# A hybrid decoder step on one core: order of loads, state products and sample work around the SSD chunks, and where the gathered rows lie

## The reference

```python
xn = _rmsnorm(x, norm_mix)
z, xbc, dt_raw, u = split(xn @ w_in)                    # 1024, 1536, 16, 1024 columns
xbc, new_conv = _causal_conv(xbc, conv_prefix, conv_w, conv_b)
y, new_ssm = _ssd_chunked(xs, dt, -exp(a_log), bm, cm, d_ssd, ssm_h0, chunk)   # 16 heads x 64, state 128
y_ssd = _rmsnorm(y * silu(z), ssd_norm)
y_s5, new_re, new_im = _s5_group(u, ...)                # recurrence, gelu, then y * sigmoid(y @ w_glu + b_glu), norm
x = x + concatenate([y_ssd, y_s5]) @ w_out
x = x + _hier_moe(_rmsnorm(x, norm_ffn), ...)           # 4 groups x 8 experts, 2 experts for each token
# inside a chunk c of the SSD part:
y_diag = einsum(cb * Lmat * dt, x)                      # products within the chunk
y_off  = einsum(C, h_prev, exp(cs))                     # from the state before the chunk
h      = decay * h + states                             # the state handed on
# inside the expert part:
h = silu(t @ w_gate[e]) * (t @ w_up[e]);  out += gates[:, e] * (h @ w_down[e])
```

## Time and profile before

| | us |
|---|---|
| median of 3 runs | 1091.96 (1091.92 to 1096.05) |
| the profiled execution, its own time | 1091.92 |
| its span in the trace | 1090.1 |
| PE busy | 982.3 (90%) |
| DVE busy | 451.7 (41%) |
| POOL busy | 332.9 (31%) |
| ACT busy | 308.8 (28%) |

### The profile page before, as it was taken

How to read it: one execution, slowest core, us unless ns; L and a number is a source line. 1 busy time by engine, 2 the same in 40 slices (tenths; PEclk the granted TensorE clock), 3 DMA queues, 4 the chain that set the end, 5 groups by cost and what they waited for, 6 DMA issues and landing times.

```text
span 1090.1 us, 17000 instructions
## 1 busy us (share of the span) xinstructions
PE 982.3 (90%) x6438; PEld 695.0 (64%) x6439; DVE 451.7 (41%) x674; ACT 308.8 (28%) x597; POOL 332.9 (31%) x534
## 2 busy tenths in 40 slices
PE   6999999999999997999999999999878778987881
PEld 5889789786776786998865555555444444544440
DVE  6999875533456998862341111111101001111103
ACT  3026223632324352231232223222211121222123
POOL 1000888888204993000012222222221111221110
PEclk9999999999999898999899999999999999999996
DMA  6674271120198534356399999999999999999954
GB/s 263 126 146 74 42 144 40 43 74 4 33 289 203 191 95 154 127 199 264 131 332 394 394 389 398 382 402 399 390 393 398 391 412 408 412 409 411 424 241 163
DMA packets 73564, 277.54 MB, mean 255 GB/s; under 512 B 36952, under 2 KB 38872, under 8 KB 56496
## 3 DMA queue, kind: packets, MB, share of 16 engines
q1 hardware_dynamic: 63020, 252.67, 63.1%
q0 software_dynamic: 8720, 19.86, 6.8%
q10 hardware_dynamic: 1780, 4.41, 1.1%
HBM read 260.17 MB, written 25.61 MB: 262 GB/s over the span
## 4 chain that ended last, share of the span: by engine, by line
PE 67%; DMA 21%; DVE 8%; issue 1%; ACT 1%; SPq 1%; ACTq 0%; POOLq 0%; POOL 0%; DVEq 0%
PE ps L658 20%; DMA sb_arena<-w_up 20%; PE ps L1026 8%; PE ps L1040 7%; PE ps L923 7%; PE ps L1019 7%; PE ps L993 2%; PE ps L777 2%; PE ps L690 1%; PE ps L803 1%; PE ps L828 1%; PE ps L746 1%; DVE sb_y_lo L1730 1%; PE ps L824 1%; DVE sb_arena L1749 1%
## 5 line engine op out<-in xcount | busy, mean ns | idle before, releaser
L658 PE MATMUL ps<-sb_arena 128*128 128x264 f32 (+1 forms) x1152 | 269.1, 395 | 9.6 <-DMA sb_arena<-wi 8.8
L658 PEld LDWEIGHTS ps<-sb_arena 128*128 128x128 f32 x1152 | 220.2, 193 | 58.6 <-DMA sb_arena<-wi 8.5
L1917 DVE TENSOR_TENSOR sb_s5b<-sb_s5b,ps 128x256 f32<-128x256 f32 x36 | 22.3, 620 | 416.2 <-PE ps L1026 416.2
L1026 PE MATMUL ps<-sb_arena 128*64 128x256 f32 x1152 | 134.6, 387 | 23.7 <-DMA sb_arena<-w_up 23.7
L1019 PE MATMUL ps<-sb_arena 128*64 128x256 f32 x1152 | 132.7, 383 | 19.6 <-DMA sb_arena<-w_gate 15.4
L1040 PE MATMUL ps<-sb_arena 128*64 128x512 f32 x576 | 131.5, 598 | 20.5 <-DVE sb_arena L1921 20.5
L1019 PEld LDWEIGHTS ps<-sb_arena 128*64 128x64 f32 x1152 | 84.0, 138 | 79.2 <-DMA sb_arena<-w_gate 25.5
L1026 PEld LDWEIGHTS ps<-sb_arena 128*64 128x64 f32 x1152 | 84.0, 139 | 70.6 <-DMA sb_arena<-w_up 30.4
L1370 ACT ACTIVATE sb_kxf<-ps,sb_gate_of 64x512 f32<-64x512 f32 x36 | 24.5, 682 | 309.9 <-PE ps L1040 309.9
L1040 PEld LDWEIGHTS ps<-sb_arena 128*64 128x64 f32 x576 | 39.2, 136 | 89.7 <-issue 60.8
L614 POOL COPY sb_idc<-sb_tok_of 64x1 int32 x36 | 6.4, 179 | 291.1 <-DMA sum_scr<-sb_kxf,sb_rwc 273.5
(11 more groups left out here) (308 smaller groups left out, 1275.9 us busy)
## 6 DMA issues: line engine op xcount, KB each, us to landing
sb_arena<-w_gate SPq DMA_DIRECT2D x32, 2048.0 KB, 33.0
sb_arena<-w_up SPq DMA_DIRECT2D x32, 2048.0 KB
sb_arena<-w_down SPq DMA_DIRECT2D x32, 2048.0 KB
sb_arena<-wi SPq DMA_DIRECT2D x28, 512.0 KB, 4.0
sb_arena<-w_out SPq DMA_DIRECT2D x4, 2048.0 KB, 7.8
sb_arena<-ssm_in POOLq DMA_DIRECT2D x8, 512.0 KB, 9.2
sb_arena<-wglu SPq DMA_DIRECT2D x8, 512.0 KB, 5.8
o_ssm_s<-sb_arena POOLq DMA_DIRECT2D x8, 512.0 KB, 3.9
```

The source lines that it names most:

```text
L658: last = mm(ps[:, b0 + h, 0:t1 - t0], ring[w % 3][:, k, :], src[:, k, t0:t1], start=k == 0, stop=k == KD - 1)
L1026: last = mm(ps[64 * r:64 * r + 64, 1, 0:256], xt[:, k, :], Wu[s][:, k, 256 * r:256 * r + 256], start=k == 0, stop=k == KD - 1)
L1917: V.tensor_tensor(hh.rearrange("p (j c) -> p c j", j=2), sg.rearrange("p (c j) -> p c j", j=2), ps[:, 1, 0:256].rearrange("p (c j) -> p c ...
```

## The change

It has seven parts, which the prediction calls by these letters.

- A. The gather targets `xg[i]` lie in partitions 0 to 63 for every i (before, odd i had partitions 64 to 127), and so do the rows of `yo`.
- B. On SP, `toeplitz(1)` stands before ring 14, and `toeplitz(2)` and `toeplitz(3)` before ring 15.
- C. On SP, `y_store(1)` stands before the wait for the first store and `y_load(0)`.
- D. On POOL, all eight sample loads stand behind the load of `bc_scr` (before, four of them stood ahead of it and two behind the second store of y). DVE waits for four loads at once.
- E. On PE, `state_outputs(0, 8)` stands after wide(24) instead of after wide(25); wide tile 27 uses bank 0; wide(29) stands behind `ssd_c(4)`; some waits go or move with that.
- F. On ACT, the gelu reads with a stride and writes in a row (before, the other way round), and four squares stand one tile later.
- G. On DVE, the scaling of `Hs` stands directly ahead of the addition to the state; the additions of rounds 0 to 7 stand in chunk 1 and those of 8 to 15 in chunk 2; two of the four sample steps that stood ahead of the wait for `y_mm` in chunk 4 stand behind it; in the tail, `root_inverse(1)` and both `scale_s5` stand before `project_out(3)`.

```diff
-        xg = [part(4288 + 1024 * i, D, p=(T * (i % 2), T * (i % 2) + T)) for i in range(RING)]
+        xg = [part(4288 + 1024 * i, D, p=(0, T)) for i in range(RING)]
@@
-        yo = [kxf[T * u:T * u + T, D + 1024 * u:D + 1024 * u + 1024] for u in range(2)]
+        yo = [kxf[0:T, D + 1024 * u:D + 1024 * u + 1024] for u in range(2)]
@@ SP
             toeplitz(0)
+            toeplitz(1)
             ring_load(14)
-            toeplitz(1)
-            ring_load(15)
             toeplitz(2)
             toeplitz(3)
-            for w in range(16, 22):
+            for w in range(15, 22):
...
+            y_store(1)
             sp.wait_ge(y5_st[0], 16 * 9)
             y_load(0)
-            y_store(1)
@@ POOL
+            pl.wait_ge(ea_out, 1)
+            pl.wait_ge(y5_mm, 16)
-            pl.wait_ge(y5_mm, 8)
-            for b in range(4, NS):
-                pl.dma_start(h0b[b], hin[b]).then_inc(h0s_ld[1], 16)
-            pl.wait_ge(ea_out, 1)
-            pl.wait_ge(y5_mm, 16)
...
-            for b in range(2):
-                pl.dma_start(h0b[b], hin[b]).then_inc(h0s_ld[0], 16)
+            for b in range(NS):
+                pl.dma_start(h0b[b], hin[b]).then_inc(h0s_ld[b // 4], 16)
             pl.wait_ge(bc_ld, 16)
-            pl.wait_ge(h0s_ld[0], 32)
-            pl.wait_ge(y5_st[1], 16 * 9)
-            for b in range(2, 4):
-                pl.dma_start(h0b[b], hin[b]).then_inc(h0s_ld[0], 16)
@@ PE
             wide(24)
+            state_outputs(0, 8)
             ssd_a(2)
+            pe.wait_ge(y5_ev, 8)
             ssd_b(2)
             ssd_y_off(2)
             wide(25)
-            pe.wait_ge(yo_ev, 4)
-            state_outputs(0, 8)
             ssd_c(2)
             state_outputs(8, 8)
...
             wide(28)
-            pe.wait_ge(yo_ev, 8)
-            wide(29)
             ssd_c(4)
-            for w in range(30, 36):
+            for w in range(29, 36):
@@ ACT
-                act_(yg[:, i, 0:NP_].rearrange("p (m j) -> p j m", j=J),
-                     yraw[:, i, 0:NP_].rearrange("p (j m) -> p j m", j=J), ACT.Gelu_apprx_tanh)
+                act_(yg[:, i, 0:NP_].rearrange("p (m j) -> p m j", j=J),
+                     yraw[:, i, 0:NP_].rearrange("p (j m) -> p m j", j=J), ACT.Gelu_apprx_tanh)
...
@@ DVE (the loop over chunks, written out)
                     else:
+                        tt(hs, hs, bc(dE[:, c, 1, 8 * g:8 * g + 8], 2, HD), ALU.mult)
                         last = V.tensor_tensor(hs, hs, pg, ALU.add)
                 last.then_inc(st_ev, 1)
-                if c == 2:
-                    s5_add(8)
+                for rd in range(8 * c - 8, 8 * c) if c in (1, 2) else ():
+                    dv.wait_ge(y5_mm, rd + 1)
...
@@ DVE, tail
             root_square(1)
-            project_out(3)
             root_inverse(1)
             scale_s5(0)
+            scale_s5(1)
+            project_out(3)
             project_out(4)
-            scale_s5(1)
```

More of the change, by code:

```diff
@@ L869, in _ @@
             ssd_a(4)
-            pe.wait_ge(wide_free[1], 14)
             ssd_b(4)
@@ L1217, in _ @@
             z_evac(20)
-            for c in range(4):
+            for c in range(5):
                 b_tokens(c)
@@ L1276, in _ @@
                         high_part(0, ySSD, PF_GSSD, k)
+                if w == 33:
                     for k in range(4, KD):
@@ L1634, in _ @@
             Ug = U[:, 0:G5 * UC].rearrange("p (g c) -> p g c", g=G5)
-            def s5_add(first):
-                for rd in range(first, first + 8):
-                    dv.wait_ge(y5_mm, rd + 1)
-                    o = Ug[:, 4 * rd:4 * rd + 4, 0:YC]
-                    V.tensor_tensor(o, o, ps[:, 2 + rd % 2, 0:4 * WIN].rearrange("p (q c) -> p q c", q=4)[:, :, 0:YC],
-                                    ALU.add).then_inc(y5_ev, 1)
-            def off_diagonal(c, n):
-                for g in range(2):
+            for c in range(5):
+                t0, n = CH[c]
+                dv.wait_ge(sa_mm, c + 1)
+                tt(cbm[0:n, :, 0:n], ps[0:n, 7, 0:256].rearrange("p (g l) -> p g l", g=2)[:, :, 0:n],
+                   bc(tri[0:n, 0:n], 1, 2), ALU.mult)
+                for q in range(2):
+                    tt(xdt[0:n, 8 * q:8 * q + 8, :], ps[0:n, 4 + q, :].rearrange("p (h d) -> p h d", d=HD),
+                       bc(dtv[0:n, c, 8 * q:8 * q + 8], 2, HD), ALU.mult)
+                dv.wait_ge(de_out, 1)
+                V.tensor_tensor(xde[0:n], xdt[0:n], bc(dE[0:n, c, 2, :], 2, HD), ALU.mult).then_inc(sa_evd, 1)
+                for g in range(2) if c else ():
                     dv.wait_ge(yo_mm, 2 * c - 1 + g)
@@ L1687, in _ @@
                     else:
+                        tt(hs, hs, bc(dE[:, c, 1, 8 * g:8 * g + 8], 2, HD), ALU.mult)
                         last = V.tensor_tensor(hs, hs, pg, ALU.add)
                 last.then_inc(st_ev, 1)
-                if c == 2:
-                    s5_add(8)
-                if c == 3:
-                    for b in range(2):
-                        sample_c(b)
-                if c == 4:
-                    for b in range(6, NS):
-                        sample_c(b)
+                for rd in range(8 * c - 8, 8 * c) if c in (1, 2) else ():
+                    dv.wait_ge(y5_mm, rd + 1)
+                    o = Ug[:, 4 * rd:4 * rd + 4, 0:YC]
+                    V.tensor_tensor(o, o, ps[:, 2 + rd % 2, 0:4 * WIN].rearrange("p (q c) -> p q c", q=4)[:, :, 0:YC],
+                                    ALU.add).then_inc(y5_ev, 1)
+                if c == 3:
+                    sample_c(0)
+                    sample_c(1)
+            for b in range(4, NS):
+                sample_c(b)
             ysi = ysm[:].rearrange("p b i -> p i b")
```

36 lines of the change are left out of this document (9 added, 27 removed).

## The result

The changed kernel takes 1102.62 us (median of 7, 1098.62 to 1104.33) where the kernel before takes 1091.92 in the same series (median of 7). The ratio is 1.0089, with a 95% interval of 1.0073 to 1.0104: about 9.7 us slower. The forecast was 1098.5, with a range of its own of 1095 to 1102: by the ratio the kernel lies just inside its upper end, by the median just above it. The profiled execution took 1102.73 us, its span is 1100.9, 10.8 more than before. Its page has PE busy for 992.9 us (before 982.3) and DVE for 441.0 (before 451.7).

The account below looks back on a forecast made before the run. The prediction took work before 560 us to reach the end one to one, then a DMA-bound weight stream; 4.2 (projection start) and 2.4 (tail) added to 1091.92 gave 1098.5 us, own range 1095 to 1102, overall range 1090 to 1109.

Parts of the forecast that it names:

- such crowding: Rival for the gathers: 64 partitions use half the DMA ports, adding 10.6 us, to 1109; chance 0.10.
- Ring 15 (part B): Before wide tile 15: PE waits 5.2 us for the later ring load, plus 2.1 of slower products, 7.3 in all.
- The recurrence: Ahead of state_outputs(0, 8): a 4.0 us wait for POOL if alone, covered by PE's delay of 7.3.
- Ring 15 lands in time: Rival before tile 15: quicker DMA issues leave only the 4.0 us wait for POOL's recurrence; 1095.2 us, chance 0.15.
- The scaling: In state_outputs(8, 8): scalings ahead of the additions of rounds 8 to 15 stall PE by 1.4; shift 8.7.
- Chunk 4: Wide(28) begins at 353.7, products for y are there at 365.8, and DVE's gate products start 6.2 us later.
- this sign of mine: Sign to look for in DVE's timeline: gate products starting at about 391.7 instead of 385.53.
- y_store(1) and y_load(0) (part C): Load lands near 349, 3 us before the first gelu, costing nothing; rival: late loads, 1101.5 us, chance 0.15.
- DVE beside POOL: DVE stage, 385 to 423 us: POOL ends 2.7 later, part of the 6.2 is given back, stage ends at 427.25.
- The tail: DVE at 448 to 463 us: projection block 5 waits 2.5 us for its bank, costing 2.4.
- The sum: Whole kernel: 4.2 plus 2.4 is 6.6 us slower, 1098.5; earlier shifts lie inside the 4.2; chance 0.50.
- The term for the projection: PE's first projection block: starts 4.2 us later, at 427.25, when the DVE stage ends.

Follow-up runs that it names:

- u_part: Changed kernel with gathered rows and result rows alternating between partitions 0 to 63 and 64 to 127 again: 1103.63 us, 1.0098 of the kernel before.
- u_scale: Changed kernel with the scaling of Hs back behind the evacuation of Yo, ahead of the chunk's products: 1096.06 us, 1.0033 of the kernel before.
- b_scale: Kernel before with only the scaling of Hs moved directly ahead of the addition to the state: 1097.61 us, ratio 1.0034.
- b_gelu: Kernel before with only the gelu changed, reading with a stride and writing in a row: 1093.90 us, ratio 0.9995.
- u_scale_store: Changed kernel with the scaling of Hs as before and y_load(0) ahead of y_store(1) again: 1097.35 us, 1.0026 of the kernel before.
- b_load: Kernel before with only the sample loads changed, all eight behind the load of bc_scr: 1086.46 us, ratio 0.9943.

## Why the prediction was right, and where it was off

- **What bounds.** Right: the shift of the first 560 us reaches the end (12.4 at the first expert, 10.8 at the end), and the expert stage keeps its length within 1.6 us. The Trainium skill (SBUF — State Buffer, "Door 1: The DMA port swizzle") has partition bit 6 pick the port of a pair, so that 64 partitions from 0 reach 8 of 16 ports. The prediction's price for such crowding, 10.6 us, was its own estimate from q0's share of the time; u_part excludes it, and no run here shows why it isn't there.
- **Ring 15 (part B).** Right in the wait, 5.14 against 5.2, and nearly in the clock, 2.5 against 2.1. PE was 8.9 us late at wide(24) instead of 7.3, of which 1.1 was there before 142 us, in a stretch that the change doesn't touch.
- **The recurrence.** Right: hidden behind the ring's delay. What I had not seen is what it would cost if it weren't hidden: I put "Ring 15 lands in time" at 1095.2, and with the wait of 3.7 us come 5.4 us of slow rounds.
- **The scaling: the term that was wrong most.** I wrote "PE stalls +1.4; the shift is 8.7". The wait was 1.29, but from 303.17 (294.27 before) to 333.58 (317.61 before, the start of wide(26)) PE lost 7.1 us, and was 16.0 late. I had charged a slow clock to waits of 3 us and more, from the earlier trace rows, and none to this short one. u_scale and b_scale show the size: 6 us at the end in the one, 4 (2 to 6) in the other.
- **Chunk 4.** I had looked for the gate products at 391.7, 6.2 us later than before; they started at 407.63, 22.1 later, so this sign of mine did not come true. Of the 15.9 us between, 10.3 lie ahead of the products for y, which DVE took at 376.10 and not at 365.8: PE was 16 us late and not 8.7, and wide(28) took 9.21 us, paced by the gelu, where I had 7.2. The other 5.6 lie behind: a wait of 2.40 us for the last products of `ssd_c(4)`, which I didn't have, and 1.6 us more each for the four sample steps and for the rest of the chain. F, which I had bounded by a gain, makes each activation of the gelu follow 0.13 us later, about 1 us of wide(28); b_gelu shows no effect of it on the time. There is also a slip in my sum: with 4.43 us of scalings taken out and 8.7 of shift, DVE is done with the small operations at 359.7 and not at 357.7, and idles 0.5 us instead of 2.5, which changes nothing behind it.
- **y_store(1) and y_load(0) (part C).** I had counted on 18.44 us for the stores and 3 us of slack. The 8 stores took 24.93 us. The slack held in the changed kernel only because PE was so late: with the scaling back, ACT waited 1.50 us for y_load(0) and PE 2.38 ahead of wide(28) (u_scale). The times don't tell u_scale from u_scale_store, so no cost of C is shown.
- **DVE beside POOL.** Right in kind: a late start is partly given back, and POOL's end is what counts. I had POOL's first update move from 344.4 to 347.1; it moved to 354.46, as sample step 0 follows PE. The projection started 11.07 later, not 4.2. DVE sets only the last 2.07 us of this: PE's last wide tile ended 16.8 us later than before (432.30 against 415.46), more than the 7.84 us that PE had waited before, so even with DVE in time the projection would have started 9.0 later. The shifts ahead of it were thus not all inside the 4.2, as I wrote. That part D in itself takes 4 to 8 us off (b_load) I had not seen: I costed it at nothing, because its loads landed in time, and I put POOL's late first update in before down to its own loads. What held it was the wait for y_store(1), 26.82 us long, released at 340.61, and D removes that. Unnamed, it is in my sum all the same: I let the first update follow sample step 0, at 347.1, and not move by the full 8.7.
- **The tail.** Right in the wait: block 5 waits 2.49 us; I had 2.5.
- **The sum.** +6.6 was forecast, +10.8 came in the traces and 1.0089 in the times. What was missing is above all the size of one term, the scaling's, with what it moves behind it. The term for the projection was 6.9 us too low; that the sum is only 4.2 too low is luck. The first products of the projection, behind a shorter wait, took 4.57 us where they had taken 5.49, and the expert stage came out 1.6 us shorter, which lies within the spread of the traces; I had neither. By the time that I gave as a sign, the stream should have come 6 to 7 us later; it came 12.4 later. That the change holds a part with a gain (D) beside those with a loss (B, G) was seen only by running them apart; alone in the kernel before, D gives 6.2, B costs 8 and the scaling 4, and what E does is open.
